# A third landing slab for the first expert stage, in the place of the residual and the position bias

## The chip, the cores and the metric

One core of a Trainium2 chip runs one program: three transformer blocks, one behind the other, on 256 tokens of width 1024, all in float32. The metric is device time in microseconds of one execution. TensorE (PE) multiplies, VectorE (DVE) and ScalarE (ACT) work element by element, GpSimd (POOL) copies and issues some transfers, SyncE (SP) issues the rest.

## The reference, cut to what matters

Block one ends with a mixture of experts: 32 experts, 4 for each token. Block two's attention adds a position bias.

```python
def moe_ffn(h, w_router, b_router, w_mlp1, b_mlp1, w_mlp2, b_mlp2):
    logits = (h @ w_router).astype(jnp.float32) + b_router.astype(jnp.float32)
    top_v, top_i = lax.top_k(logits, TOP_K)
    gates = jax.nn.softmax(top_v, axis=-1)
...
        u = xb @ w_mlp1[e] + b_mlp1[e]
        x_glu = jnp.minimum(u[..., ::2], SWIGLU_LIMIT)
        x_lin = jnp.clip(u[..., 1::2], -SWIGLU_LIMIT, SWIGLU_LIMIT)
        a = x_glu * jax.nn.sigmoid(SWIGLU_ALPHA * x_glu) * (x_lin + 1)
        return a @ w_mlp2[e] + b_mlp2[e]
...
        y = moe_ffn(h.reshape(B * S, D), w_router[l], b_router[l], w_mlp1[l], b_mlp1[l],
                    w_mlp2[l], b_mlp2[l]).reshape(B, S, D)
        x = x + gt2 * rms_norm(y, g_post_ffn[l])
...
        s_c = jnp.einsum('bthd,bnd->bhtn', qb, kc) + tab[:, rel_bucket(dist_c)][None]
```

The second line from the end shows that the residual `x` is needed again only when all experts are summed. `tab[:, rel_bucket(...)]` is the position bias of block two; it depends on no activation.

## The kernel before, in words

**The expert stage.** The 1024x2048 and 1024x1024 weights of one expert are cut into six slabs of 2 MB: 0 to 3 (w_mlp1) and 4, 5 (w_mlp2). Each has one place in SBUF: 0, 1 and 2 in `ring`, 3 in `MOD`, 4 in `HTY`, 5 in `scr`. A place may be loaded again when TensorE has used it in the expert's last pass (semaphore `m1_slab_used[j]`). A pass takes 32 of the expert's tokens; an expert with more has several passes, and all of them need all six slabs. How many passes each expert has is counted on the chip by VectorE (a list that it makes at the stage's start, semaphores `counted` and `listed`); the loops over experts (SP, POOL) and over passes (PE, DVE, ACT) run on those numbers.

Slabs 0 and 1 have a second place each, a landing slab in `scr` (`m1_arrivals`). SP loads the next expert's slabs 0 and 1 there while the present one is still at work, and POOL copies them into `ring` when `m1_slab_used` allows (L712), then tells TensorE by `moved[j]`. SP's order for one expert e is: 2, 3, the bias row, 4, 5 of e, then 0 and 1 of e + 1, each behind its own wait (`next_expert`). One queue carries them in this order.

**One pass on TensorE** (`expert_pass`): up-projection over slabs 0 to 3 (L1111) and the bias row (L1115), the scatter of the pass before (L1148), `back` (L1094), the transposes of the hidden tile (`turn_hidden`, L1124), `gather` for the next pass (L1079), then the down-projection with slabs 4 and 5 (L1137). Between L1115 and L1124 stand, on VectorE, two clamps out of PSUM (L2249, L2250), the multiply by the sigmoid (L2252) and the product with the linear half (L2253), whose result L1124 turns.

**The position bias.** A one-hot product makes one row of 512 distances per head, which ScalarE stores to DRAM (`rel_scratch`). POOL loads windows of it: `BIASR` in one transfer (L689) and `BIASCR` in eight transfers of single elements, every sixteenth (L693). TensorE turns them round with the matrix `flip` in five products (L1021, L1023; plan entry `flip`, behind `gate1`), ScalarE copies the results to `BIAS` and `BIASC`. Block one does not use them.

**Between the expert stage and block two.** POOL waits for the last sum, then loads the parameters of block two (L715 to L720, semaphore `block2_params_landed`, 6 transfers) and clears two areas. TensorE waits for VectorE's new residual (`x1_ready`) and for all six transfers, then turns X (L776) and begins the projections `in2`.

Of the kernel before, what the change touches and what calls it, by code (L numbers as in the profile page):

```python
# [12 lines left out]
P = 128  # L13
S = 256
# [136 lines left out]
def build(nc, I, out, rel_scratch):  # L151
    first, end, first_slab, release = product_plan()
    landed = landed_plan()
    with ExitStack() as ctx:
# [101 lines left out]
        moved, moving = [sem(f"moved{j}") for j in range(2)], sem("moving")  # L256
        early_landed = slab_landed[SLOTS:]
        m1_landed = [sem(f"m1_landed{i}") for i in range(6)]
        m1_row_landed = sem("m1_row_landed")
# [38 lines left out]
        m1_arrivals = [carve(1024 + SLAB * j, 2, 2 * F1) for j in range(2)]  # L298
        b1row, YS = borrow(1024, BANK), borrow(1536, BANK)
# [141 lines left out]
        n_first, n_rel, n_consts = 4, 3, 24  # L441
# [4 lines left out]
        def _(sp):  # L446
# [183 lines left out]
        def _(pool):  # L630
# [16 lines left out]
            with nc.allow_non_contiguous_dma("short vectors"):  # L647
                vector(0)
                const(flip, I["c_flip"], rel_consts_landed)
# [36 lines left out]
            pool.memset(KN, 0.0).then_inc(zeros_ready, 1)  # L686
            pool.wait_ge(rel_stored, 16)
# [7 lines left out]
            vector(3)  # L695

            pool.wait_ge(h2_ready, NT)
            for a in range(NT):
                for half in range(2):
                    r = E1 * (2 * a + half)  # L700
                    pool.dma_start(b2row[r:r + E1, :], I["b_mlp2"][0][:, BANK * half:BANK * (half + 1)]).then_inc(moe1_params_landed, 16)
            for j in range(2):
                pool.wait_ge(early_landed[j], 16 + 16)
                pool.sem_inc(moved[j], 1)
            pool.wait_ge(m1["counted"], 1)
            with pool.Fori(1, E1) as e:
                through = pool.value_load(work[0:1, bass.ds(e + (THROUGH - 1), 1)], min_val=1, max_val=PASSES)
                for j in range(2):
                    pool.wait_ge(m1_landed[j], 16 * e)
                    pool.wait_ge(m1_slab_used[j], through)  # L710
                    pool.sem_inc(moving, 1)
                    pool.tensor_copy(m1_slabs[j], m1_arrivals[j]).then_inc(moved[j], 1)  # L712

            pool.wait_ge(m1["sum"], 1)
# [17 lines left out]
            for j in range(2):  # L732
                pool.wait_ge(early_landed[j], 32 + 32)
                pool.sem_inc(moved[j], 1)
# [11 lines left out]
        def _(pe):  # L746
# [275 lines left out]
            b = bank()  # L1022
            close(pe.matmul(b[:, 0:NT * 4 * NCMP], flip, BIASCR, start=True, stop=True))  # L1023
# [74 lines left out]
            def up(n, e):  # L1098
# [3 lines left out]
                for j in range(4):  # L1102
                    if j < 2:
# [5 lines left out]
                    for i in range(2):  # L1109
                        for c in range(STRIPS1):  # L1110
# [91 lines left out]
            for i in range(4):  # L1202
# [8 lines left out]
                if i in (0, 3):  # L1211
                    tokens(lambda k: wi[:, k, S:2 * S], S)

# [267 lines left out]
        def _(act):  # L1481
# [150 lines left out]
            for i in range(4):  # L1632
                read(BIAS[:, 2 * i:2 * i + 2, :], two(product()))
            read(BIASC[:, :, :, :].rearrange("p t h n -> p (t h n)"), product()[:, 0:NT * 4 * NCMP])
# [96 lines left out]
            read(GH[:, :, :], two(product()), ACT.Sigmoid)  # L1731
            act.wait_ge(conv_gated, 1)
# [130 lines left out]
        def _(dve):  # L1863
# [277 lines left out]

            attention(0, n_window, between_windows)
# [142 lines left out]
            gain_gate(5)  # L2285
            add_gated_norm(Y, 5, m1["sum_read"], NT)
# [51 lines left out]

            attention(n_window, n_window + n_nsa, between_units)
# [224 lines left out]
```

## Time and profile before

| | us |
|---|---|
| runs: median of 3 (lowest, highest) | 2499.62 (2497.68, 2503.69) |
| the profiled execution, its own time | 2493.21 |
| its span in the trace | 2491.4 |
| TensorE busy | 2062.1 (83%) |
| POOL busy | 320.4 (13%) |
| chain that ended last | PE 63%, DMA 22%, DVE 9% |

The three blocks follow one another: the expert stage of block one lies between about 280 and 1283 us of the span, block two follows. Busy shares are means over stages with different limits. A row of the timeline gives start, duration, engine, line, operation and tiles; in brackets stand the idle time before it and what ended it. Names such as `scr<-in_w_mlp` are destination and source.

### The profile page before, as it was taken

Reading aid. Unit: us, or ns where it says so; the run is one execution under the profiler, and the core shown is the slowest. Engines: PE = TensorE matmul, PEld = TensorE weight load, DVE = VectorE, ACT = ScalarE, POOL = GpSimd, SP = SyncE. Lnnn points to the kernel's source line nnn. Section 1 sums busy time; section 2 is a strip of 40 time slices with the busy share of each in tenths; the row PEclk is TensorE's granted clock in tenths of the full one; section 3 lists DMA queues with packets and bytes.
Section 4 is the critical chain, followed back from the end, with each engine's and each line's share of the span. In section 5 each row is a group of like instructions: output and inputs, shape, how many; then the busy total and the mean of one; then the engine's idle time right before and its main releaser. Section 6 shows DMA issues by size and latency. Waiting matters only on the chain.

```text
span 2491.4 us, 34823 instructions
## 1 busy us (share of the span) xinstructions
PE 2062.1 (83%) x14301; PEld 1148.7 (46%) x14302; DVE 521.0 (21%) x1100; ACT 367.3 (15%) x815; POOL 320.4 (13%) x147
## 2 busy tenths in 40 slices
PE   6988589668768966989869788899979899889788
PEld 5765222112212211222228665789965546555444
DVE  1044511001101100111120473110031201241131
ACT  1232111001101100111111422100001112210001
POOL 4100112222222122211220000000000000002221
PEclk9978699889999988999989979999979999989889
DMA  9653679999999799997983635555524334259994
GB/s 322 166 204 140 270 305 401 427 425 409 424 419 408 306 426 426 391 407 311 413 327 136 224 121 200 177 158 144 157 89 139 115 127 161 77 227 383 409 410 162
DMA packets 183290, 681.49 MB, mean 274 GB/s; under 512 B 15954, under 2 KB 57187, under 8 KB 150192
## 3 DMA queue, kind: packets, MB, share of 16 engines
q1 hardware_dynamic: 179200, 670.02, 69.0%
q0 software_dynamic: 4000, 10.37, 1.7%
q8 instruction: 59, 0.97, 0.2%
q14 instruction: 15, 0.12, 0.0%
q10 hardware_dynamic: 16, 0.02, 0.0%
HBM read 679.31 MB, written 1.06 MB: 273 GB/s over the span
## 4 chain that ended last, share of the span: by engine, by line
PE 63%; DMA 22%; DVE 9%; ACT 3%; SPq 2%; issue 1%; POOL 0%; DVEq 0%; ACTq 0%; POOLq 0%
PE ps L765 32%; PE ps L1111 9%; DMA spare<-in_b_mlp 8%; DMA scr<-in_w_mlp 6%; DMA MOD<-in_w_mlp 5%; PE ps L1137 4%; PE ps L1416 2%; PE ps L1148 2%; DMA HTY<-in_w 2%; PE ps L800 2%; PE ps L1115 1%; PE ps L1079 1%; PE ps L1453 1%; DVE scr L2316 1%; PE ps L1427 1%
## 5 line engine op out<-in xcount | busy, mean ns | idle before, releaser
L1111 PE MATMUL ps<-ring,scr 128*32 128x512 f32 x2208 | 286.6, 666 | 133.1 <-POOL ring L712 132.7
L765 PE MATMUL ps<-ring,HTY 128*128 128x512 f32 (+5 forms) x960 | 327.8, 502 | 7.0 <-DMA ring<-in_w_out 3.9
L712 POOL COPY ring<-scr 128x4096 f32<-128x4096 f32 x62 | 224.0, 3617 | 776.2 <-DMA scr<-in_w_mlp 570.1
L765 PEld LDWEIGHTS ps<-ring,HTY 128*128 128x128 f32 x960 | 175.3, 191 | 156.0 <-issue 141.1
L765 PE MATMUL ps<-HTY,ring 128*128 128x256 f32 (+1 forms) x1072 | 238.0, 385 | 1.8 <-ACT HTY L1500 1.8
L1111 PEld LDWEIGHTS ps<-ring,scr 128*32 128x32 f32 x2208 | 72.2, 118 | 342.3 <-POOL ring L712 180.2
L765 PEld LDWEIGHTS ps<-HTY,ring 128*128 128x128 f32 (+1 forms) x1072 | 205.3, 192 | 33.2 <-ACT HTY L1500 2.8
L2249 DVE TENSOR_SCALAR spare<-ps 128x256 f32<-128x256 f32 x46 | 19.5, 424 | 679.4 <-PE ps L1115 679.3
L1500 ACT ACTIVATE scr<-ps 128x512 f32<-128x512 f32 (+6 forms) x118 | 58.4, 497 | 498.3 <-PE ps L765 401.2
L1111 PE MATMUL ps<-MOD,scr 128*32 128x512 f32 x736 | 98.9, 659 | 39.3 <-DMA spare<-in_b_mlp 20.2
L765 PE MATMUL ps<-ring,scr 128*128 128x128 f32 (+1 forms) x1040 | 121.6, 280 | 1.4 <-DVE scr L2355 1.4
L765 PEld LDWEIGHTS ps<-ring,scr 128*128 128x128 f32 x1040 | 117.5, 192 | 5.2 <-issue 3.3
L1674 ACT ACTIVATE spare<-spare 128x256 f32<-128x256 f32 x46 | 19.1, 416 | 597.0 <-DVE spare L2249 597.0
L742 POOL COPY scr<-MOD 128x4096 f32<-128x4096 f32 x7 | 25.2, 3600 | 565.3 <-PE ps L1416 451.9
L1416 PE MATMUL ps<-scr,BIAS 128*32 128x512 f32 x432 | 73.4, 677 | 23.5 <-POOL scr L742 22.8
L1137 PE MATMUL ps<-scr 128*32 128x512 f32 x736 | 88.5, 598 | 5.0 <-DMA scr<-in_w_mlp 5.0
L1148 PE MATMUL ps<-spare,scr 64*128 64x512 f32 x368 | 91.4, 615 | 0.8 <-ACT spare L1684 0.8
L1137 PE MATMUL ps<-HTY,scr 128*32 128x512 f32 x736 | 89.7, 606 | 0.0
L765 PEld LDWEIGHTS ps<-spare,H 128*128 128x128 f32 x320 | 75.4, 329 | 9.2 <-issue 7.5
L765 PE MATMUL ps<-spare,H 128*128 128x128 f32 x320 | 77.3, 402 | 1.6 <-DVE spare L2470 1.6
L1111 PEld LDWEIGHTS ps<-MOD,scr 128*32 128x32 f32 x736 | 24.3, 117 | 104.2 <-issue 64.7
L844 PE MATMUL ps<-ring,cols 128*32 128x128 f32 x1472 | 53.0, 304 | 18.5 <-DMA ring<-in_w_ada 18.5
(443 smaller groups left out, 1982.7 us busy)
## 6 DMA issues: line engine op xcount, KB each, us to landing
scr<-in_w_mlp SPq DMA_DIRECT2D x94, 2048.0 KB, 25.5
ring<-in_w_mlp SPq DMA_DIRECT2D x34, 2048.0 KB, 21.0
MOD<-in_w_mlp SPq DMA_DIRECT2D x32, 2048.0 KB, 24.3
HTY<-in_w_mlp SPq DMA_DIRECT2D x32, 2048.0 KB, 22.2
ring<-in_w_ada SPq DMA_DIRECT2D x23, 2048.0 KB, 9.4
ring<-in_w_in SPq DMA_DIRECT2D x20, 2048.0 KB, 7.9
ring<-in_w_ff SPq DMA_DIRECT2D x16, 2048.0 KB, 9.0
ring<-in_w SPq DMA_DIRECT2D x16, 2048.0 KB, 16.2
```

The costliest lines, as they stand in the source:

```text
L712: pool.tensor_copy(m1_slabs[j], m1_arrivals[j]).then_inc(moved[j], 1)
L742: pool.tensor_copy(m3_slabs[j], m3_arrivals[j]).then_inc(moved[j], 1)
L765: mm = pe.matmul(o, lhs(k), rhs(k), start=begin and k == 0, stop=end and k == nk - 1)
L800: mm = pe.matmul(b[64 * half:64 * half + 64, S * i:S * (i + 1)], c[half](k), rhs[:, k, :], start=k == 0, stop=k == nk - 1)
L844: pe.matmul(b[32 * t:32 * (t + 1), 0:P], csil[:, j, k:k + 1].to_broadcast([P, 32]), w[:, k, P * t:P * (t + 1)], start=k == 0, stop=False)
L1079: mm = pe.matmul(ps[C1 * q:C1 * (q + 1), 3, 0:S], PICK[:, a, :], H[:, a, S * q:S * (q + 1)], start=a == 0, stop=a == NT - 1)
L1111: mm = pe.matmul(ps[C1 * c:C1 * (c + 1), 0, :], XG[:, 2 * j + i, :], m1_slabs[j][:, i, BANK * c:BANK * (c + 1)], start=j + i == 0, stop=False)
L1115: mm = pe.matmul(ps[C1 * c:C1 * (c + 1), 0, :], ones[32 * c:32 * c + 1, 0:C1], b1row[32 * c:32 * c + 1, :], start=False, stop=True)
L1137: mm = pe.matmul(ps[r:r + C1, 1, :], aT[:, i, C1 * c:C1 * (c + 1)], m1_slabs[j][:, 2 * t + i, BANK * half:BANK * (half + 1)], start=j + i ...
L1148: mm = pe.matmul(sum_bank(a, half), GPT[r, P * a:P * (a + 1)], YS[r, :], start=False, stop=last, skip_group_check=True)
L1416: mm = pe.matmul(ps[32 * t:32 * (t + 1), 0, :].rearrange("p (x f) -> p x f", x=2), XG3[:, 4 * h + i, C3 * t:C3 * (t + 1)], m3_slabs[2 * h ...
L1500: act.activation(dst, src, func, **kw).then_inc(product_free, 1)
```

## The change

The residual X and the table BIAS together are as large as one slab. The change makes them a third landing place, for slab 2, in two halves of 1 MB (row pairs k = 0 into X, k = 1 into BIAS). So X is stored to DRAM (`x_scratch`) at the start of the stage and loaded back at its end, and the bias is made in block two: its loads stand on POOL's queue after the last sum, and the plan entry `flip` behind `in2`. SP's order for one expert becomes 3, row, 4, 5 of e, then 0, 1 and the two halves of 2 of e + 1. POOL makes four copies for each expert. VectorE has three waits more (for `rel_stored`, for X, and for `flip` before block two's attention).

```diff
-    ("ada1a", [2] * 4, 0), ("rel", [], 1), ("h1T", [], 4), ("in1", [2, 3, 2, 2, 2], 0), ("gate1", [], 1), ("flip", [], 5),
+    ("ada1a", [2] * 4, 0), ("rel", [], 1), ("h1T", [], 4), ("in1", [2, 3, 2, 2, 2], 0), ("gate1", [], 1),
...
-    ("x1T", [], 4), ("convw", [], 1), ("in2", [4, 3, 2, 2, 2, 2], 0), ("cmp2", [1, 1], 3), ("ada3", [2] * 6, 7), ("ada3b", [2] * 2, 3),
+    ("x1T", [], 4), ("convw", [], 1), ("in2", [4, 3, 2, 2, 2, 2], 0), ("flip", [], 5), ("cmp2", [1, 1], 3), ("ada3", [2] * 6, 7), ("ada3b", [2] * 2, 3),
...
+        m1_half_arrivals = [X.rearrange("p a d -> p (a d)"), BIAS.rearrange("p h s -> p (h s)")]
...
+            def expert_half(e, k, dst, landed=None):
+
+                src = I["w_mlp1"][0][e][4 * P:6 * P, :].rearrange("(p k) n -> p k n", p=P)
+                landed = (m1_landed[2], m1_half_landed)[k] if landed is None else landed
+                sp.dma_start(dst, src[:, k, :]).then_inc(landed, 16)
...
-                for j in (2, 3):
-                    sp.wait_ge(m1_slab_used[j], through)
-                    expert_slab(own, j)
+                sp.wait_ge(m1_slab_used[3], through)
+                expert_slab(own, 3)
...
+                    for k in range(2):
+                        sp.wait_ge(moved[2 + k], e + 1)
+                        expert_half(behind, k, m1_half_arrivals[k])
...
-            expert_slab(0, 2)
+            for k in range(2):
+                expert_half(0, k, m1_slabs[2][:, k, :], early_landed[k])
             sp.wait_ge(h2_ready, NT)
             expert_slab(0, 3)
             expert_row(0)
+            sp.dma_start(x_scratch, X[:, :, :]).then_inc(x_stored, 16)
+            expert_half(1, 1, m1_half_arrivals[1])
             sp.wait_ge(product_ready, end["route1"])
             expert_slab(0, 4)
+            sp.wait_ge(x_stored, 16)
+            expert_half(1, 0, m1_half_arrivals[0])
             sp.wait_ge(m1["counted"], 1)
...
+            sp.wait_ge(moved[2], E1)
+            sp.dma_start(X[:, :, :], x_scratch).then_inc(x_landed, 16)
...
+                for k, landed_half in enumerate((m1_landed[2], m1_half_landed)):
+                    pool.wait_ge(landed_half, 16 * e)
+                    pool.wait_ge(m1_slab_used[2], through)
+                    pool.sem_inc(moving, 1)
+                    pool.tensor_copy(m1_slabs[2][:, k, :], m1_half_arrivals[k]).then_inc(moved[2 + k], 1)
+
+            pool.wait_ge(m1["sum"], 1)
+            pool.dma_start(flip, I["c_flip"]).then_inc(rel_landed, 16)
...
-            pe.wait_ge(rel_landed, 16 * (1 + 4 * NT))
-            for i in range(4):
-                b = bank()
-                close(pe.matmul(b, flip, BIASR[:, 2 * i:2 * i + 2, :], start=True, stop=True))
...
+            dve.wait_ge(x_landed, 32)
             add_gated_norm(Y, 5, m1["sum_read"], NT)
...
+            dve.wait_ge(product_free, end["flip"])
             attention(n_window, n_window + n_nsa, between_units)
```

POOL's queue at the end of the expert stage, before. The first row is the copy of slabs 0 and 1 in the loop over experts; the loads behind the branch are the parameters of block two.

```order
L712 COPY ring<-scr 128x4096 x2
L706 REGISTER_ALU
L706 COMPARE_AND_BRANCH
L715 DMA scr<-in_nsa_cmp_w_2 128x4x64
L716 DMA scr<-in_conv_pw_w 128x2x256
L717 DMA scr<-in_conv_dw_w 31x256
L719 DMA scr<-in_nsa_cmp_b_2 1x16x16 x2
L720 DMA scr<-in_b_ada 48x128
```

The same place of the changed kernel (its lines are numbered anew).

```order
L722 COPY ring<-scr 128x4096 x2
L727 COPY ring<-X 128x2048
L727 COPY ring<-BIAS 128x2048
L716 REGISTER_ALU
L716 COMPARE_AND_BRANCH
L730 DMA scr<-in_c_flip 128x128
L733 DMA scr<-rel_scratch 128x8x256
L737 DMA scr<-rel_scratch 128x15x1 x8
L739 DMA scr<-in_nsa_cmp_w_2 128x4x64
L740 DMA scr<-in_conv_pw_w 128x2x256
L741 DMA scr<-in_conv_dw_w 31x256
L743 DMA scr<-in_nsa_cmp_b_2 1x16x16 x2
```

Two copies are added in the loop, and ten loads now stand ahead of block two's parameters; in the kernel before nine of them followed the loading of constants in block one, and `flip` was among those.

TensorE behind `in1`, before: the gate product (L1016), the five flip products, and the first scores of attention (L881).

```order
L1016 MATMUL ps<-scr,wgu 128x256 x2
L1021 MATMUL ps<-scr 128x512 x4
L1023 MATMUL ps<-scr 128x120
L881 MATMUL ps<-spare,scr 128x256 x4
L844 MATMUL ps<-ring,cols 32x128 x32
```

And TensorE of the changed kernel behind the last product of `in2` (L789), ahead of the products `cmp2` (L1249), where the five now stand.

```order
L789 MATMUL ps<-HTY,ring 128x256 x32
L1237 MATMUL ps<-scr 128x512 x4
L1239 MATMUL ps<-scr 128x120
L1249 MATMUL ps<-ring,scr 15x128 x32
L1252 MATMUL ps<-scr,ones 15x128 x2
```

The five products moved from between the gate and the first scores to between `in2` and `cmp2`.

## Rows read from the trace of the kernel before

**Rows 1.** Windows: busy us (x instructions) of PE, PEld, DVE, ACT, POOL; clock, DMA share, GB/s

```profile
405.00:1255.00 850.00, 659.83 (x5178) 198.72 (x5170) 117.18 (x312) 99.28 (x234) 193.03 (x55) 0.92 0.96 400
825.00:855.00 30.00, 28.87 (x252) 9.51 (x248) 5.51 (x16) 5.09 (x12) 7.14 (x2) 1.00 0.43 173
```

**Rows 2.** Timeline of POOL, copies of slab 0 of two experts that follow

```profile
642.28 3.60 POOL L712 COPY ring<-scr 128x4096 f32<-128x4096 f32 x1 [21.14 <-DMA scr<-in_w_mlp]
...
671.95 3.60 POOL L712 COPY ring<-scr 128x4096 f32<-128x4096 f32 x1 [21.27 <-DMA scr<-in_w_mlp]
```

**Rows 3.** Timeline of SP, issue of slab 2 and slab 4 after a long hole

```profile
842.83 0.34 SPq L489 DMA_DIRECT2D ring<-in_w_mlp  x1
...
851.58 0.39 SPq L491 DMA_DIRECT2D HTY<-in_w_mlp  x1
```

**Rows 4.** Timeline of an expert's end, its slab-1 copy beside VectorE's multiply

```profile
585.59 3.60 POOL L712 COPY ring<-scr 128x4096 f32<-128x4096 f32 x1 [1.20 <-DMA scr<-in_w_mlp]
...
586.56 2.90 DVE L2252 TENSOR_TENSOR spare<-spare 128x256 f32<-128x256 f32 x1
...
589.98 0.51 PE L1124 MATMUL ps<-ident,spare 128*128 128x128 f32 x2 [2.24 <-DVE spare L2253]
```

**Rows 5.** Timeline at the stage's start, VectorE's list of passes beside POOL's first copies

```profile
283.42 8.17 POOL L712 COPY ring<-scr 128x4096 f32<-128x4096 f32 x2 [22.23 <-issue]
...
284.39 3.73 DVE L2234 TENSOR_TENSOR spare<-spare,rows 128x1056 f32<-128x1056 f32 x1
...
298.93 0.70 PE L1124 MATMUL ps<-ident,spare 128*128 128x128 f32 x2 [10.48 <-DVE spare L2253]
...
304.68 0.40 SPq L491 DMA_DIRECT2D HTY<-in_w_mlp  x1
```

**Rows 6.** Timeline of an expert's end where both slabs had landed early

```profile
839.46 7.14 POOL L712 COPY ring<-scr 128x4096 f32<-128x4096 f32 x2 [36.13 <-PE ps L1111]
...
848.17 0.48 PE L1124 MATMUL ps<-ident,spare 128*128 128x128 f32 x2 [0.56 <-ACT scr L1670]
```

**Rows 7.** Timeline after the last sum: parameters of block two, turn of X

```profile
1282.34 0.80 POOL L715 DMA_DIRECT2D scr<-in_nsa_cmp_w  x1 [21.00 <-PE ps L1148]
...
1285.38 0.51 POOL L720 DMA_DIRECT2D scr<-in_b_ada  x1
...
1294.40 1.97 PE L776 MATMUL ps<-ident,X 128*128 128x128 f32 x8 [12.38 <-DVEq L2287]
```

**Rows 8.** Timeline of POOL in block one, loads of the bias; last, line L693's landing

```profile
55.55 0.90 POOL L689 DMA_DIRECT2D scr<-rel_scratch  x1
...
68.58 5.97 POOL L693 DMA_DIRECT2D scr<-rel_scratch  x5 [9.73 <-issue]
83.53 1.20 POOL L693 DMA_DIRECT2D scr<-rel_scratch  x1 [8.97 <-issue]
84.73 0.56 POOL L645 DMA_DIRECT2D spare<-in_g_post_ffn  x1
...
DMA to landing us min/median/max: 7.0/8.2/16.0
```

**Rows 9.** Window over those loads, columns as in rows 1

```profile
70.00:76.00 6.00, 6.00 (x30) 5.28 (x29) 0.00 (x0) 0.60 (x1) 4.55 (x4) 1.00 0.91 56
```

**Rows 10.** Timeline: flip products on TensorE, the first scores read by VectorE

```profile
113.19 2.84 PE L1021 MATMUL ps<-scr 128*128 128x512 f32 x6
119.28 1.84 PE L1021 MATMUL ps<-scr 128*128 128x512 f32 x2 [3.25 <-ACT BIAS L1500]
120.91 0.62 PE L1023 MATMUL ps<-scr 128*128 128x120 f32 x2
...
120.26 1.42 DVE L2111 TENSOR_TENSOR_SCAN scr<-ones,scr 128x256 f32<-128x256 f32 x2
...
123.28 0.88 DVE L1978 SCALAR_TENSOR_TENSOR scr<-ps,window 128x256 f32<-128x256 f32 x2 [1.61 <-PE ps L881]
```

**Rows 11.** Timeline of TensorE behind `in2`

```profile
1393.47 2.75 PE L1222 MATMUL ps<-ring,scr 128*15 128x128 f32 x24 [4.13 <-DVE scr L2296]
```

More of the change, by code:

```diff
@@ L255, in build @@
         m1_slab_used = [sem(f"m1_slab_used{j}") for j in range(6)]
-        moved, moving = [sem(f"moved{j}") for j in range(2)], sem("moving")
+        moved, moving = [sem(f"moved{j}") for j in range(4)], sem("moving")
         early_landed = slab_landed[SLOTS:]
         m1_landed = [sem(f"m1_landed{i}") for i in range(6)]
+        m1_half_landed, x_stored = sem("m1_half_landed"), sem("x_stored")
         m1_row_landed = sem("m1_row_landed")
@@ L439, in slot @@
             return shaped(places[place(s)][:, off:off + k * n], (k, n))
-        n_first, n_rel, n_consts = 4, 3, 24
+        n_first, n_rel, n_consts = 4, 2, 24
         first_gains = (2, 3, 0, 1)
@@ L648, in _ @@
                 vector(0)
-                const(flip, I["c_flip"], rel_consts_landed)
                 const(onehot, I["c_onehot"], rel_consts_landed)
@@ L686, in _ @@
             pool.memset(KN, 0.0).then_inc(zeros_ready, 1)
+            vector(3)
+            pool.wait_ge(h2_ready, NT)
+            for a in range(NT):
+                for half in range(2):
+                    r = E1 * (2 * a + half)
+                    pool.dma_start(b2row[r:r + E1, :], I["b_mlp2"][0][:, BANK * half:BANK * (half + 1)]).then_inc(moe1_params_landed, 16)
+            for j in range(2):
+                pool.wait_ge(early_landed[j], 16 + 32)
+                pool.sem_inc(moved[j], 1)
+                pool.sem_inc(moved[2 + j], 1)
+            pool.wait_ge(m1["counted"], 1)
+            with pool.Fori(1, E1) as e:
+                through = pool.value_load(work[0:1, bass.ds(e + (THROUGH - 1), 1)], min_val=1, max_val=PASSES)
+                for j in range(2):
+                    pool.wait_ge(m1_landed[j], 16 * e)
+                    pool.wait_ge(m1_slab_used[j], through)
+                    pool.sem_inc(moving, 1)
+                    pool.tensor_copy(m1_slabs[j], m1_arrivals[j]).then_inc(moved[j], 1)
+                for k, landed_half in enumerate((m1_landed[2], m1_half_landed)):
+                    pool.wait_ge(landed_half, 16 * e)
+                    pool.wait_ge(m1_slab_used[2], through)
+                    pool.sem_inc(moving, 1)
+                    pool.tensor_copy(m1_slabs[2][:, k, :], m1_half_arrivals[k]).then_inc(moved[2 + k], 1)
+            pool.wait_ge(m1["sum"], 1)
+            pool.dma_start(flip, I["c_flip"]).then_inc(rel_landed, 16)
             pool.wait_ge(rel_stored, 16)
@@ L694, in _ @@
                             .then_inc(rel_landed, 16)
[L695 to L714, printed above, removed]
             pool.dma_start(cw2, I["nsa_cmp_w2_2"][0].rearrange("a (c p) n -> p a c n", p=P)).then_inc(block2_params_landed, 16)
@@ L732, in _ @@
             for j in range(2):
-                pool.wait_ge(early_landed[j], 32 + 32)
+                pool.wait_ge(early_landed[j], 48 + 32)
                 pool.sem_inc(moved[j], 1)
@@ L1017, in _ @@
             close(mm)
-            pe.wait_ge(rel_landed, 16 * (1 + 4 * NT))
-            for i in range(4):
-                b = bank()
-                close(pe.matmul(b, flip, BIASR[:, 2 * i:2 * i + 2, :], start=True, stop=True))
-            b = bank()
-            close(pe.matmul(b[:, 0:NT * 4 * NCMP], flip, BIASCR, start=True, stop=True))
             def rest_of_modulation(i):
@@ L1102, in up @@
                 for j in range(4):
-                    if j < 2:
+                    if j < 3:
                         pe.wait_ge(moved[j], e + 1)
@@ L1109, in up @@
                     for i in range(2):
+                        if 2 * j + i == 5:
+                            pe.wait_ge(moved[3], e + 1)
                         for c in range(STRIPS1):
@@ L1212, in _ @@
                     tokens(lambda k: wi[:, k, S:2 * S], S)
+            pe.wait_ge(rel_landed, 16 * (2 + 4 * NT))
+            for i in range(4):
+                b = bank()
+                close(pe.matmul(b, flip, BIASR[:, 2 * i:2 * i + 2, :], start=True, stop=True))
+            b = bank()
+            close(pe.matmul(b[:, 0:NT * 4 * NCMP], flip, BIASCR, start=True, stop=True))
             pe.wait_ge(blocks_ready, 1)
@@ L1631, in _ @@
             log_sigmoid_part(GL[:, :, :], GZ[:, :, :])
-            for i in range(4):
-                read(BIAS[:, 2 * i:2 * i + 2, :], two(product()))
-            read(BIASC[:, :, :, :].rearrange("p t h n -> p (t h n)"), product()[:, 0:NT * 4 * NCMP])
             def rest_of_modulation(i):
@@ L1731, in _ @@
             read(GH[:, :, :], two(product()), ACT.Sigmoid)
+            for i in range(4):
+                read(BIAS[:, 2 * i:2 * i + 2, :], two(product()))
+            read(BIASC[:, :, :, :].rearrange("p t h n -> p (t h n)"), product()[:, 0:NT * 4 * NCMP])
             act.wait_ge(conv_gated, 1)
@@ L2140, in between_windows @@
                     merge(0, end["ada1b"])
+            dve.wait_ge(rel_stored, 16)
             attention(0, n_window, between_windows)
```

1 line of the change is left out of this document (added).

## The prediction

> **What bounds the kernel now.** I read the page first: TensorE is busy 83% of the span and the chain of work that ended last gives 22% to transfers. An average over three blocks says little about one stage, so I cut the first expert stage out by windows. From 405 to 1255 us the 16 DMA engines are busy 96% and move 400 GB/s [rows 1]. The reader is to see two regimes. In the first, POOL begins the copy of slab 0 every 29.6 us [rows 2]: six slabs of 2.10 MB in that time are 425 GB/s, and TensorE waits for transfers. In the second, an expert has two or more passes, every buffer is full, and DMA runs dry. At 425 GB/s the 850 us could have moved 6% more, so DMA is idle for 850 x 25/425 = 50 us; one long hole holds 17.8 of it (30 us at 173 GB/s) [rows 1], and the other, from 1140 to 1170, is like it. A third landing slab is aimed at these 50 us.
>
> **Part 1, the landing slab: what it can give.** When a pass frees buffers, SyncE issues slab 2 (842.83) and, 8.75 us later, slab 4 (851.58) [rows 3]; slab 3 goes between them. DMA needs 4.93 us a slab (29.6/6), so slabs 2 and 3 keep it busy for 9.86 us, and slab 4 starts 1.1 us after it could have by its own wait. In the changed kernel slab 2 is already in the residual's and the bias' place. DMA then restarts on slab 3, which ends before slab 4 may be issued. What follows the hole (slabs 4 and 5, then 0 and 1 of the next expert) is tied to slab 4's buffer, that is to TensorE's last use of it. The lead of 4.93 us is spent inside the hole; only 1.1 us per hole comes out. I count eleven ends of expert with full buffers. At most eight of them pass on to DMA a restart that is set by slabs 2 and 3, and where the next expert also has several passes TensorE alone sets the pace and nothing is gained.
>
> **Part 2, the landing slab: what it costs.** Each expert now gets four POOL copies: two of 3.60 us and two halves, by size 1.8 us each. While transfers are the bound they are hidden: they end 3.6 + 3.6 = 7.2 us after slab 1 landed, slab 3 lands after 9.9. At the end of a multi-pass expert they are not. The vector multiply at L2252 reads two SBUF tiles. In most passes it takes 0.42 us; in seven it takes more, 2.90 in the one shown, and each time it ends 0.27 us after POOL's copy (585.59 + 3.60; 586.56 + 2.90) [rows 4]. So it waits for POOL. The next instruction, L2253, also reads two SBUF tiles, and TensorE's transposes at L1124 wait for it: in that pass they sat idle 2.24 us. With a half copy queued behind slab 1's copy, L2252 slips in between (at 284.39 a waiting vector instruction did just that: it ended at 288.12, inside POOL's pair, and the pair took 8.17 us instead of 7.14 [rows 5, 6]). Then the half goes, and L2253 waits 1.8 us for it. No row shows L2253 itself beside a copy: bounds are nothing (it waits for nobody) and 3.6 us (both halves first). I take 1.8, by the nearest row, L2252, which has the same kinds of operands.
>
> The Trainium skill speaks against the change here (SBUF — State Buffer, "Who interferes with whom"): "A DVE instruction with two SBUF inputs contends with a GpSimd instruction that reads SBUF", and whichever starts first keeps the shared port for its whole instruction. By that rule L2253 waits as L2252 does; the trace agrees for L2252 with its 2.90 us. Were the rule limited to L2252, the loop term below would be -2 instead of +14.
>
> The ledger of the loop, by ends of expert. (a) Four with both copies back to back, like 839.46: L2252 just escapes, and the transposes at 848.17 have waited for ScalarE, so 0.8 us of the 1.8 is slack [rows 6]: 1.0 lost, 1.1 gained, about 0; at the first of them the next expert is TensorE's again and there is no gain: +1.0. (b) Seven where L2252 already waits, like 585.59: no slack. In two of them (near 585 and 676) slab 4 already set the restart: +1.7 each. In two more 1.1 and 1.4 remain after the gain. Three are followed or made by multi-pass experts in a row (1023 to 1090): 1.8, 1.4 and 0.3. Sum of (b): 9.4. (c) The start. There the pair at 283.42 stands beside VectorE's list of passes; L2234 took 3.73 us, and L1124 waited 10.48 us for VectorE, slab 4 of expert 1 being issued only at 304.68 [rows 5]. Two more halves, 2 x 1.8 us, meet the rest of that list, some fifteen short instructions from L2236 to L2258, nearly all with two SBUF tiles or a copy from SBUF to SBUF: +3.5, with DMA idle meanwhile, so it is passed on whole. Loop: 1.0 + 9.4 + 3.5 = **+14 us**; bounds -2 (L2253 free) and +23 (eleven times 1.8, plus 3.5, no gain).
>
> Hidden at nothing: the store of the residual (1.05 MB) and expert 1's halves, in the DMA hole before 304.68; and the reload, queued behind the last expert's slab 5, while VectorE adds the residual only after the last sum, where POOL too moves on at 1282.34 [rows 7] (2.5 us of transfer; without that cover it costs those 2.5).
>
> **Part 3, the bias moves to block two.** (a) Its ten loads now stand on POOL's queue after the sum and *ahead* of the six that TensorE waits for before it turns X. Before, these were issued from 1282.34 to 1285.9 and TensorE turned X at 1294.40, having waited for VectorE alone [rows 7]. In block one POOL needed 29.2 us from the window load at 55.55 to its next work at 84.73: the eight loads of single elements pause twice, 9.73 and 8.97 us [rows 8]. That is issue only; from 70 to 76 DMA is busy 91% at 56 GB/s [rows 9], so these loads also hold the engines. Low bound: no pause. 1282.34 + 0.56 + 0.90 + 8 x 1.20 = 1293.4, the last parameter load 3.0 later, landing at least 7.0: 1303.4, +9. High bound: both pauses, landing 16.0 [rows 8]: 1282.9 + 29.2 + 3.0 + 16.0 = 1331, +37. Between: from 68.58 to 83.53 five loads drained before POOL moved again, 3.0 us each; eight are 24, the window load 2.5 at 425 GB/s, from 1283.8 to 1310.3, and the parameters land 7.0 later: 1317.3. TensorE begins 22.9 later than now: **+23 us**. Nothing gives it back: behind TensorE stand ScalarE's reads, and the next slabs are released by its products. (b) Five flip products in block one go. They ran from 113.19, and VectorE's first score read came at 123.28 instead of at 121.7, when its scan ended [rows 10]: **-1.5**. (c) They return after in2, where TensorE sits idle 4.13 us for VectorE [rows 11]; they need 2.84 + 1.84 + 0.62 = 5.3 [rows 10]: **+1.2**. Without that hole it would be 5.3.
>
> **Sum.** 14 + 23 - 1.5 + 1.2 = 36.7 us. The profiled execution took 2493.21 (span 2491.4 and 1.8 around it), so it would take 2529.9. It is 6.4 under the median of the runs shown, 2499.62; forecast as such a median: **2536.3**.
>
> **Rivals.** *L2253 waits for nobody* (0.16). For it: no row shows it beside a copy. Against: its operands. Loop -2: 2520.5. *POOL's queue runs through* (0.13). For it: in block one 24 constants stood in the queue ahead of these loads; here none do. Against: the second pause came after only five loads. Params +9: 2522. *The lead is kept* (0.05): a stall is shortened by a whole slab, 4.93 us in each of three long holes (the third lies near 360) and the short ones whole, 50 - 2 x 17.8 = 14.4: 29 us; with 3.5, 23, 1.2 and -1.5 beside it 2497, not slower. It needs slab 4 not to be tied to TensorE's last use. Against: 851.58 less 842.83 is only 8.75. It decides once more than 26 us come out. *The wait for parameters nears its high bound* (0.08): 2552 and up.
>
> **Numbers.** My forecast has 0.58, and its own range is 2524 to 2548. The range 2514 to 2552 takes in both milder rivals and leaves out the kept lead and the high bound, some 0.15. A change of 0.3% (7.5 us) can be told from none: slower 0.94, within it 0.03, faster 0.03.
>
> **What would show it.** TensorE's turn of X after a wait of more than 20 us that ends on a parameter load; POOL's eight element loads with one or two pauses after the sum; L2252 at 0.4 and L2253 late by about 1.8 in passes with a half copy; slab 4 of expert 1 issued near 308 (less 1.5); the holes as long in TensorE's time but with 2.1 MB less to load after them. I am wrong if the element loads drain in a few us, or if the time from one slab-4 issue to the next shrinks by more than 2 us at the end of multi-pass experts.

## The result and the profile after

| | before | after |
|---|---|---|
| median, us | 2498.65 | 2531.32 (2524.12 to 2532.87) |
| ratio | | 1.0133, 95% interval 1.0116 to 1.0150 |
| the profiled execution, its span | 2493.21, 2491.4 | 2531.37, 2529.6 |

The change makes the kernel 1.3% slower. The forecast was 2536.3, in a range from 2514 to 2552.

The page of the changed kernel: busy times, and three groups of its fifth part.

```profile
PE 2075.8 (82%) x14301; PEld 1153.5 (46%) x14302; DVE 541.5 (21%) x1100; ACT 367.6 (15%) x815; POOL 438.8 (17%) x209
...
L722 POOL COPY ring<-scr 128x4096 f32<-128x4096 f32 x62 | 223.8, 3617 | 673.3 <-DMA scr<-in_w_mlp 486.8
...
L1144 PE MATMUL ps<-ident,spare 128*128 128x128 f32 x92 | 22.9, 332 | 58.6 <-DVE spare L2281 39.4
```

POOL is busy 118 us more (its half copies take 61.3 and 60.8), which by itself costs nothing. The last row does: TensorE's transposes (L1144, before L1124) now wait 39.4 us for VectorE's L2281, where they waited 18.4 for L2253 before; their whole wait grew from 41.0 to 58.6. Next, windows over the same 850 us as [rows 1], with the same columns.

```profile
405.00:1255.00 850.00, 660.25 (x5132) 195.85 (x5125) 131.56 (x304) 96.72 (x228) 297.51 (x108) 0.92 0.94 393
```

The third landing slab was to fill the gaps between transfers, and DMA moves less than before: 393 GB/s for 400.

**An expert's end with several passes**, answering to [rows 4]: POOL, VectorE and TensorE of the changed kernel.

```profile
589.00 3.60 POOL L722 COPY ring<-scr 128x4096 f32<-128x4096 f32 x1 [1.29 <-DMA scr<-in_w_mlp]
592.54 2.08 POOL L727 COPY ring<-X 128x2048 f32<-128x2048 f32 x1
594.57 2.08 POOL L727 COPY ring<-BIAS 128x2048 f32<-128x2048 f32 x1
...
589.97 2.90 DVE L2280 TENSOR_TENSOR spare<-spare 128x256 f32<-128x256 f32 x1
592.91 1.99 DVE L2281 SCALAR_TENSOR_TENSOR spare<-spare 128x256 f32<-128x256 f32 x1
...
594.96 0.70 PE L1144 MATMUL ps<-ident,spare 128*128 128x128 f32 x2 [3.82 <-DVE spare L2281]
```

The reader is to see a chain of hand-overs. L2280 ends at 592.87, 0.27 after slab 1's copy; the first half starts at 592.54; L2281 ends at 594.90, again 0.28 after that copy. An instruction of 0.42 us lasts nearly as long as its neighbour. TensorE's wait grew from 2.24 to 3.82.

The wait has a tail. Windows over the 35 products that follow it, first here, then at the same end in the kernel with late copies (below), where TensorE waits 0.56:

```profile
594.96:599.50 4.54, 4.54 (x35) 1.56 (x35) 0.82 (x3) 0.77 (x2) 1.69 (x1) 0.66 0.49 208
```

```profile
584.17:587.30 3.13, 3.13 (x35) 1.23 (x35) 1.58 (x1) 0.77 (x2) 3.13 (x2) 1.00 1.04 442
```

The third number from the end is TensorE's granted clock, a share of 2.4 GHz: 0.66 behind the long wait, 1.00 without it. The same products take 1.4 us more.

And the end where both slabs had landed early, answering to [rows 6] and [rows 3].

```profile
848.26 7.14 POOL L722 COPY ring<-scr 128x4096 f32<-128x4096 f32 x2 [32.35 <-PE ps L1131]
855.35 2.16 POOL L727 COPY ring<-X 128x2048 f32<-128x2048 f32 x1
...
855.79 1.99 DVE L2281 SCALAR_TENSOR_TENSOR spare<-spare 128x256 f32<-128x256 f32 x1
...
857.84 0.51 PE L1144 MATMUL ps<-ident,spare 128*128 128x128 f32 x2 [1.34 <-DVE spare L2281]
...
853.44 0.33 SPq L492 DMA_DIRECT2D MOD<-in_w_mlp  x1
...
861.29 0.39 SPq L494 DMA_DIRECT2D HTY<-in_w_mlp  x1
```

Here 0.56 of the wait is the usual one for ScalarE, so 0.78 is lost. DMA restarts on slab 3 at 853.44 and slab 4 follows 7.85 later, still tied to TensorE.

**The start**, answering to [rows 5]: VectorE's list of passes beside four copies, and slab 4 of expert 1.

```profile
283.64 8.17 POOL L722 COPY ring<-scr 128x4096 f32<-128x4096 f32 x2 [21.91 <-issue]
291.76 1.89 POOL L727 COPY ring<-X 128x2048 f32<-128x2048 f32 x1
293.60 1.89 POOL L727 COPY ring<-BIAS 128x2048 f32<-128x2048 f32 x1
...
291.90 1.80 DVE L2266 TENSOR_SCALAR spare<-spare,stat 128x66 f32<-128x66 f32 x1
293.73 1.83 DVE L2267 TENSOR_TENSOR spare<-spare 128x66 f32<-128x66 f32 x1
...
308.34 0.41 SPq L494 DMA_DIRECT2D HTY<-in_w_mlp  x1
```

Each half stretches one short instruction (0.32 and 0.23 us before) to its own length.

**The end of the stage**, answering to [rows 7]: POOL's loads, then TensorE's turn of X.

```profile
1294.91 0.57 POOL L730 DMA_DIRECT2D scr<-in_c_flip  x1 [17.47 <-PE ps L1168]
1295.48 0.92 POOL L733 DMA_DIRECT2D scr<-rel_scratch  x1
1296.38 8.38 POOL L737 DMA_DIRECT2D scr<-rel_scratch  x7
1318.42 1.20 POOL L737 DMA_DIRECT2D scr<-rel_scratch  x1 [13.66 <-issue]
1319.62 0.76 POOL L739 DMA_DIRECT2D scr<-in_nsa_cmp_w  x1
...
1322.63 0.51 POOL L744 DMA_DIRECT2D scr<-in_b_ada  x1
...
1328.17 3.65 PE L800 MATMUL ps<-ident,X 128*128 128x128 f32 x16 [33.57 <-issue]
```

Seven loads of single elements go through, the eighth waits 13.66, and the six parameters stand behind it. TensorE is idle 33.57 us where it was idle 12.38.

**In block one**, where the flip products stood ([rows 10]): TensorE, then a window of 119 to 126 us of before and of after (0.50 is the lower of the two levels, 1.2 GHz, for the whole window).

```profile
122.64 2.08 PE L905 MATMUL ps<-spare,scr 128*128 128x256 f32 x4 [8.32 <-DVE scr L2005]
124.65 3.06 PE L868 MATMUL ps<-ring,cols 128*32 128x128 f32 x64
```

```profile
119.00:126.00 7.00, 5.68 (x40) 3.47 (x44) 4.57 (x11) 3.72 (x9) 0.00 (x0) 0.76 0.04 13
```

```profile
119.00:126.00 7.00, 3.36 (x32) 2.43 (x36) 4.75 (x12) 2.78 (x10) 0.00 (x0) 0.50 0.04 15
```

### The profile page after: what moved, and what is told of

It is laid out like the page before. It is cut to its first block, busy times and chain, and to the rows that moved or that the text cites. A ratio compares the mean times of both kernels' runs of the same rounds, so it can differ in the third digit from the quotient of the medians.

```text
span 2529.6 us, 35042 instructions
## 1 busy us (share of the span) xinstructions
PE 2075.8 (82%) x14301; PEld 1153.5 (46%) x14302; DVE 541.5 (21%) x1100; ACT 367.6 (15%) x815; POOL 438.8 (17%) x209
## 4 chain that ended last, share of the span: by engine, by line
PE 61%; DMA 22%; DVE 9%; ACT 3%; issue 2%; SPq 2%; POOL 0%; DVEq 0%; ACTq 0%; POOLq 0%
PE ps L789 32%; DMA scr<-in_w_mlp 17%; PE ps L1131 7%; PE ps L1157 5%; PE ps L1443 2%; DMA spare<-in_b_mlp 2%; PE ps L824 2%; DMA HTY<-in_w 1%; PE ps L1097 1%; PE ps L1168 1%; PE ps L1135 1%; PE ps L1480 1%; PE ps L1454 1%; PE ps L868 1%; PE ps L930 1%
## 5 line engine op out<-in xcount | busy, mean ns | idle before, releaser
L1131 PE MATMUL ps<-ring,scr 128*32 128x512 f32 x2208 | 296.7, 682 | 134.8 <-POOL ring L722 128.2
L789 PE MATMUL ps<-ring,HTY 128*128 128x512 f32 (+5 forms) x960 | 328.0, 503 | 7.0 <-DMA ring<-in_w_out 4.0
L789 PEld LDWEIGHTS ps<-ring,HTY 128*128 128x128 f32 x960 | 175.3, 191 | 156.2 <-issue 141.3
L789 PE MATMUL ps<-HTY,ring 128*128 128x256 f32 (+1 forms) x1072 | 238.1, 385 | 1.8 <-ACT HTY L1527 1.8
L789 PEld LDWEIGHTS ps<-HTY,ring 128*128 128x128 f32 (+1 forms) x1072 | 205.4, 192 | 33.2 <-ACT HTY L1527 2.7
L2277 DVE TENSOR_SCALAR spare<-ps 128x256 f32<-128x256 f32 x46 | 19.5, 425 | 670.2 <-PE ps L1135 670.2
L789 PE MATMUL ps<-ring,scr 128*128 128x128 f32 (+1 forms) x1040 | 121.6, 280 | 1.4 <-DVE scr L2385 1.4
L789 PEld LDWEIGHTS ps<-ring,scr 128*128 128x128 f32 x1040 | 117.5, 192 | 5.2 <-issue 3.3
L1131 PE MATMUL ps<-MOD,scr 128*32 128x512 f32 x736 | 89.3, 603 | 20.2 <-DMA spare<-in_b_mlp 14.8
L789 PEld LDWEIGHTS ps<-spare,H 128*128 128x128 f32 x320 | 75.4, 329 | 9.2 <-issue 7.5
L789 PE MATMUL ps<-spare,H 128*128 128x128 f32 x320 | 77.3, 402 | 1.6 <-DVE spare L2500 1.6
L1144 PE MATMUL ps<-ident,spare 128*128 128x128 f32 x92 | 22.9, 332 | 58.6 <-DVE spare L2281 39.4
```

The costliest lines, as they stand in the source:

```text
L789: mm = pe.matmul(o, lhs(k), rhs(k), start=begin and k == 0, stop=end and k == nk - 1)
L1131: mm = pe.matmul(ps[C1 * c:C1 * (c + 1), 0, :], XG[:, 2 * j + i, :], m1_slabs[j][:, i, BANK * c:BANK * (c + 1)], start=j + i == 0, stop=False)
```

## Three intervals that make all runs comparable

Executions of one kernel differ by some 10 us, and half of that arises before the expert stage: POOL's first copy begins anywhere from 278.6 to 284.1 us in kernels that have the same code up to there. So I cut each profiled execution at three points: POOL's first copy, POOL's first load after the last sum, and TensorE's turn of X; the rest is up to the end of the span. The first row comes out of [rows 5, 7], the second from the rows above (1294.91 - 283.64, 1328.17 - 1294.91, 2529.6 - 1328.17), the others in the same way from their traces.

| kernel | expert stage | load to turn | turn to end | median, us | ratio (95%) |
|---|---|---|---|---|---|
| before | 998.92 | 12.06 | 1197.0 | 2498.65 | |
| after | 1011.27 | 33.26 | 1201.4 | 2531.32 | 1.0133 |
| e1_loads_last | 1011.25 | 12.07 | 1199.2 | 2507.65 | 1.0042 (1.0028, 1.0057) |
| e2_bias_only | 1000.74 | 31.59 | 1203.4 | 2515.80 | 1.0070 (1.0053, 1.0087) |
| e3_halves_late | 990.21 | 33.01 | 1202.2 | 2507.99 | 1.0043 (1.0029, 1.0057) |
| e4_copies_late | 980.22 | 32.66 | 1202.4 | 2498.68 | 1.0005 (0.9993, 1.0016) |
| e5_both | 979.88 | 12.06 | 1203.3 | 2475.79 | 0.9922 (0.9904, 0.9940) |
| e6_before_late | 989.37 | 12.06 | 1200.9 | 2483.15 | 0.9949 (0.9930, 0.9967) |
| e7_four_loads | 1011.32 | 24.09 | 1200.8 | 2518.13, one run | |
| e8_both_clock | 979.91 | 12.06 | 1199.8 | 2486.14 | 0.9956 (0.9940, 0.9972) |
| e9_psum_operand | 994.47 | 33.36 | 1198.2 | 2511.42 | 1.0057 (1.0042, 1.0072) |
| e10_both_clock_7 | 979.69 | 12.06 | 1199.8 | 2478.38 | 0.9917 (0.9902, 0.9932) |

The reader is to see how sharp the first two columns are, and where they are not. Kernels that share the stage's code agree within 0.1 us (1011.25 to 1011.32) and 0.6 us (979.69 to 980.22), whatever their whole times do. But e2_bias_only has the stage's code of before and takes 1.8 us more (1000.74 for 998.92): of its seven stalls of L2252 five last 2.87 to 2.89 us, in before only two do. So what is measured against the stage of before is known to some 2 us. The runs beside which each kernel was timed had medians of 2497.50 (e1 to e4), 2496.63 (e5 to e8) and 2497.63 (e9, e10).

## The experiments

**Is it the queue ahead of the parameters?** In the changed kernel the bias loads were moved behind the parameters and the clears.

```diff
-            pool.dma_start(flip, I["c_flip"]).then_inc(rel_landed, 16)
...
             for area in (BD, KN):
                 pool.memset(area, 0.0).then_inc(zeros_again, 1)
+            pool.dma_start(flip, I["c_flip"]).then_inc(rel_landed, 16)
...
```

> The changed kernel, only the ten loads of the bias moved on POOL's queue: behind block two's six parameters and the two clears. Theory (parameters late because they queue behind the element loads, issue and transfer together): TensorE's turn of X again waits for VectorE, near 1307 instead of 1328.17, so 21 us come back: about 2510. The bias is then made under in2's 95 us, and TensorE does not wait for it ahead of the flip products. Rival (the same transfers only delay something else later, such as the weights of in2): less than half comes back, 2520 or more, with waits for weights between 1310 and 1400. Rival (the turn waits for something else, such as the reload of X): no change, 2531.

TensorE's turn of X stands at 1302.18 after 12.38 us for VectorE; the interval is 12.07 as before, and the stage is the same. The eighth load still pauses (11.18 us), with nobody behind it who matters. The wait costs 33.26 - 12.07 = 21.2 us and nothing is taken elsewhere.

**Does the move of the bias cost this without the landing slab?** The kernel before with part 3 of the change alone.

```diff
             pool.wait_ge(m1["sum"], 1)
+            pool.dma_start(flip, I["c_flip"]).then_inc(rel_landed, 16)
...
             pool.dma_start(cw2, I["nsa_cmp_w2_2"][0].rearrange("a (c p) n -> p a c n", p=P)).then_inc(block2_params_landed, 16)
```

> The kernel before with only the bias moved to block two, its loads ahead of the parameters as in the changed kernel; no third landing slab, no store or reload of X. Theory (the two halves of the change add up): parameters +21, block one +0.5 (the 1.5 gained turns into a loss because TensorE's clock falls), blocks two and three +4.4: 26 slower than before, about 2525. The element loads pause near 13.7 us again. Rival (the wait of 33.6 us ahead of the turn comes from the landing slab, whose reload and last transfers are in the way of the loads): under 15 slower, 2513 or less.

Load to turn 31.59, which is 19.5 more than before (the pause was 12.21). The whole is 18 us slower, not 26: I had put 4.4 into blocks two and three and 0.5 into block one from one pair of profiles, and no cost of that size shows. The last column runs from 1197.0 to 1203.4 in the twelve kernels whatever their code there, and e6_before_late, whose code there is that of before, has 1200.9. The rival is out.

**Is it L2281 beside the halves, and L2280 beside slab 1?** POOL waits for the expert's last hidden tile before the halves, and in the second kernel before slab 1's copy already.

```diff
+                pool.wait_ge(m1["hidden"], through)
                 for k, landed_half in enumerate((m1_landed[2], m1_half_landed)):
```

```diff
                     pool.wait_ge(m1_slab_used[j], through)
+                    if j == 1:
+                        pool.wait_ge(m1["hidden"], through)
```

> The changed kernel, with POOL waiting for VectorE's L2281 of the expert's last pass (semaphore hidden) before it copies the two halves; slabs 0 and 1 as before. Theory (L2281 waits for the copy of the first half, and TensorE for L2281): all L2281 take 0.42 us, where twelve took 1.99; 12 x 1.57 = 18.8 less the slack in five of them (0.8 each) and less what slab 4's restart then gives up, and the start gives back its 3.5: about 15 come out of the loop, 2516. Rival (L2281's wait is hidden; what costs is the split of a slab into two transfers, or POOL being late with the halves): within 4 of 2531.

> As the run with late halves, but POOL waits for hidden already before the copy of slab 1, so that no copy but slab 0's can stand beside L2280 and L2281. Theory (L2280's stalls of 0.45 to 2.5 us in seven passes, which the kernel before has too, cost TensorE as much): another 8 to 10 us, 2507, and L2280 takes 0.42 throughout. Rival (the copies then come too late for TensorE's next up-projection): TensorE waits for moved at slab 1 or 2, and the time is that of the late halves or worse.

With late halves the stage loses 21.1 us (1011.27 to 990.21), more than the 15 expected; L2281 is never longer than 0.43 (it was 1.99 eleven times; my expectation says twelve, a miscount). With slab 1's copy late as well another 10.0 us go, to 980.22, and both take 0.42 throughout. TensorE does not wait for the later copies at these ends. VectorE's L2281 and TensorE at the end shown above, in the kernel with both edits (L2283, L1146 there), beside the late copies:

```profile
580.39 3.60 POOL L724 COPY ring<-scr 128x4096 f32<-128x4096 f32 x1 [3.40 <-DVE spare L2283]
583.93 2.08 POOL L729 COPY ring<-X 128x2048 f32<-128x2048 f32 x1
...
579.71 0.42 DVE L2283 SCALAR_TENSOR_TENSOR spare<-spare 128x256 f32<-128x256 f32 x1
582.53 1.73 DVE L2207 TENSOR_TENSOR spare<-spare 128x256 f32<-128x256 f32 x1 [2.40 <-PE ps L1099]
```

The copy now follows L2283 at once. What is stretched in its place is L2207 (0.43 to 1.73), for which no other engine waits.

**Is it that both inputs lie in SBUF?** Copies as in the changed kernel; L2281 reads one input from PSUM.

```diff
-                    pe.wait_ge(m1["up_read"], n)
+                    pe.wait_ge(m1["hidden"], n)
...
-                tell(dve.scalar_tensor_tensor(aS, lin1, 1.0, sig, ALU.add, ALU.mult), m1["hidden"], n + 1)
+                tell(dve.scalar_tensor_tensor(aS, ps[:, 0, 1:BANK:2], 1.0, sig, ALU.add, ALU.mult), m1["hidden"], n + 1)
```

> The changed kernel, only L2281 reads the linear half from PSUM, so that it has one SBUF input instead of two (the clamp L2278 still runs, but its limit at 7 is left out of the product; TensorE frees the bank at hidden instead of at up_read). POOL's copies stay as they are. Theory (it waits because both its inputs are in SBUF, as POOL's copy is): L2281 takes 0.42 to 0.5 also beside a half copy, L2280 still waits 2.9 beside slab 1's; the loop is as with the late halves, about 20 us shorter, 2511. Rival (any vector instruction, or any that writes SBUF, waits for the copy): L2281 stays at 1.99 in twelve passes, 2531.

The same end of expert in this kernel: POOL, and VectorE's two instructions.

```profile
582.15 3.60 POOL L722 COPY ring<-scr 128x4096 f32<-128x4096 f32 x1 [1.29 <-DMA scr<-in_w_mlp]
585.70 2.09 POOL L727 COPY ring<-X 128x2048 f32<-128x2048 f32 x1
...
583.12 2.90 DVE L2280 TENSOR_TENSOR spare<-spare 128x256 f32<-128x256 f32 x1
586.06 0.42 DVE L2281 SCALAR_TENSOR_TENSOR spare<-ps,spare 128x256 f32<-128x256 f32 x1
```

L2280, with both inputs in SBUF, still takes 2.90 beside slab 1's copy. L2281, with one, runs in 0.42 in the middle of the half copy at 585.70. On VectorE only the place of one operand was changed (with it TensorE's release of the bank came later, and the clamp dropped out of the product), and 16.8 us of the stage went (1011.27 to 994.47; I had expected 20). That is the price of the eleven waits. The trace agrees with the rule that the prediction quoted of the Trainium skill (SBUF — State Buffer, "Who interferes with whom"): with two inputs in SBUF the instruction waits, 2.90 us, and with one it does not, 0.42.

**What the third slab gives when it is not in the way.** The kernel before, with the wait ahead of slab 1's copy (the second diff above), and the changed kernel with both edits.

> The kernel before, two landing slabs, with only the wait for hidden ahead of slab 1's copy. Theory (L2252's stalls beside slab 1's copy, 10.4 us over seven passes, stand on TensorE's path): L2252 takes 0.42 in all passes, the loop is 8 us shorter, 2490; what the third slab itself gives is then the rest of the 18.7 us that the late copies took out of the loop of before, about 10. Rival (the stalls were slack, or slab 1 then comes late): within 3 of before, and the third slab has given nearly all of the 18.7.

> The changed kernel with both edits: slab 1's copy and the two halves behind hidden, and the bias loads behind the parameters. Theory (two causes, in different stages, that add): the loop as with the late copies, 980.2 us from POOL's first copy to the last sum (998.9 before), and TensorE's turn of X 12.1 behind POOL's first load: 33 and 21 us less than the changed kernel, about 2477, faster than the kernel before by 21. Rival (block two was short of POOL or of DMA time either way): more than 2487.

Before gains 9.6 us of stage and 0.5% of its time from one line. The third slab then gives 9.5 more (989.37 to 979.88), and in the whole time 2483.15 to 2475.79. The kernel with both edits is 0.8% faster than the kernel before and 2.2% faster than the change. Its DMA in the stage:

```profile
405.00:1240.00 835.00, 662.47 (x5162) 196.12 (x5158) 140.06 (x308) 98.12 (x231) 298.41 (x110) 0.91 0.97 406
```

**Issue or transfer?** Four of the eight element loads are left out, and with them half of `BIASCR`; TensorE waits for four loads fewer, and its last flip product reads `BIASR` instead. The kernel serves for this interval alone.

```diff
-                for t in range(NT):
+                for t in range(1):
                     for h in range(4):
```

> The changed kernel with four of the eight loads of single elements (half of BIASCR is left out, and the last flip product reads other data). Theory (the loads hold the DMA engines as well as POOL's queue): POOL does not pause, the parameters are issued 19 us earlier, but land only when the four have drained, at 3.0 each: the turn of X waits for parameters until about 15 us behind POOL's first load, some 18 earlier than with eight loads, and 3 later than without them. Rival (only the pause of the queue cost time): the turn waits for VectorE alone, 12.1 behind the first load. Second rival (the pause is not a matter of how many loads stand there): a pause of 9 or more among or behind the four.

POOL does not pause: the last parameter is issued at 1300.67, 9.3 us behind the first load (with eight 27.7), yet TensorE turns X only at 1315.48. Load to turn is 24.09: half of the loads keep 12.0 of the 21.2 us. From 1300 to 1305 DMA is busy and moves little:

```profile
1300.00:1305.00 5.00, 0.00 (x0) 0.00 (x0) 2.10 (x2) 0.00 (x0) 5.00 (x8) 0.50 1.00 76
```

So the rival that only the queue's pause cost time is out. My own number for this run, 15, was too low: I had counted the elements alone, and in the same stretch stand the window load of 1 MB and slabs of in2 (368 GB/s from 1310 to 1316).

**Did the clock eat the 1.5 us of block one?** Filler products where the flip products stood, on top of both edits; first fifteen, then seven.

```diff
+            b = bank()
+            for i in range(15):
+                pe.matmul(b, ident[:, :], X[:, 0, 0:BANK], start=True, stop=True)
```

> As the run with both edits, and in block one, where the flip products stood, 15 products of the same size into a bank that nobody reads before its next product overwrites it. Theory (without the flip products TensorE is idle for 8.3 us and its granted clock falls to 0.50 from 119 to 126, where it was 0.76; this turned the 1.5 us gained into 0.5 lost): the clock stays above 0.9 there, L868's first 64 products take 1.95 where they took 3.06, and TensorE is about 2 us earlier by 130. In the whole time 2 us are below what the ratio can tell. Rival (the loss is from the order of TensorE and ScalarE, not from the clock): the clock rises, and the time by 130 stays as it is or gets later.

> As the run with both edits and filler products in block one, but seven products instead of fifteen: each has two entries in the trace and takes 0.88 us, so that fifteen took 13.1 us and delayed the first scores by 6.5; seven take 6.1, inside TensorE's 8.3 idle us. Theory (the clock ate the 1.5 us): granted clock 1.00 from 119 to 126 instead of 0.50, L870's first 64 products take 1.95, and TensorE is 1 to 2 us earlier at the second group of them than with both edits alone; in the whole time no difference that the ratio can tell, 2474 against 2476. Rival (what the clock is granted between 130 and 280 depends on how TensorE stood before, and undoes it): POOL's first copy comes as late as in the run with fifteen, 14.8 us behind that with both edits, or anywhere between.

Fifteen were a mistake of size: they took 13.14 us and pushed the first scores behind VectorE. By 154 us VectorE was 5.2 late, by 192 it was 6.9, and POOL's first copy came 14.8 late; most of the rest fell where the clock from 190 to 220 was 0.66 instead of 0.89. Behind the fifteen the first 64 products took 1.95, so at that place the clock was kept. Seven fit:

```profile
113.63 6.28 PE L1047 MATMUL ps<-X,ident 128*128 128x512 f32 x14
119.74 1.03 PE L907 MATMUL ps<-spare,scr 128*128 128x256 f32 x4
123.09 1.13 PE L907 MATMUL ps<-spare,scr 128*128 128x256 f32 x4 [2.32 <-DVE scr L2011]
124.15 3.46 PE L870 MATMUL ps<-ring,cols 128*32 128x128 f32 x64
```

```profile
119.00:122.50 3.50, 1.77 (x7) 0.83 (x5) 3.01 (x6) 1.46 (x2) 0.00 (x0) 1.00 0.13 51
122.50:128.00 5.50, 4.91 (x76) 3.87 (x76) 3.31 (x10) 1.74 (x9) 0.00 (x0) 0.69 0.01 3
```

The filler kept the clock at 1.00 to 122.5 and it fell right after: the 64 products took 3.46, longer than without filler. From the gate product to the second group of 64 it is 16.96 us, with both edits alone 17.01, before 16.91. My theory that seven products give the 1.5 us back fails; with them the low stretch moved and did not go. POOL's first copy stands at 284.65, 4.2 behind both edits alone, as the rival allowed. The time shows nothing (2478.38 and 2475.79, intervals overlapping).

## Why the prediction was right, step by step

- **The loop, +14: measured +12.35** (1011.27 - 998.92; 10.5 against e2_bias_only, with the same stage as before), and in the main from the right parts. *The start*, +3.5: the first to the second copy of slab 0 took 43.87 us for 40.44, +3.4 (42.21, 43.56 and 43.82 in e1, e7 and e9, whose copies there are the same); with late halves it is 40.41. *The waits*: eleven, as counted, at 1.57 each instead of 1.8, since L2281 took 1.99 and needs 0.42; 0.78 instead of 1.0 where ScalarE's result leaves slack. By the kernel with the PSUM operand they cost 16.8; my eleven less slack were 7 x 1.8 + 4 x 1.0 = 16.6. That these two agree is in part luck: with the sizes measured the sum is 7 x 1.57 + 4 x 0.78 = 14.1. What it lacks, and the prediction had at nothing, is *the clock behind a long wait*. At the five ends where TensorE waited 2.87 to 3.82 us, it took 4.95 to 6.38 us from the transposes to the second half of the down-projection, where it takes 3.59 at full clock: 9.2 in all. With the PSUM operand these ends lost 5.0, in before 1.7. TensorE's wait for the hidden tile is 11.8 less with the PSUM operand (58.6 and 46.8), the slow products 4.2 less: 16.0 of the 16.8. *What the slab gives back*: 20.2 less 12.35 is 7.9; the ledger had 6.1 in it. With no copy in VectorE's way it gives 9.5, of at most 8 x 1.1 = 8.8 that I had allowed. The lead of a whole slab is not kept: 31 ends of expert give 9.5 us, less than two slabs' 4.93.
- **Single ends** were less good than their sum. By the times of slab 0's copies the two ends near 369 and 401 bring -0.9, those at 839 and 1159 -0.8 each, where I had +1.0 for the four (the -0.9 is one long interval of before, 45.46, for 44.5 in every other kernel). The seven others bring +9.9 for 9.4, but as 1.4, 2.9, 1.1, 3.3, 0.8, -0.4 and 0.9: the sum is right, and luck has a part in it. At two of them (1063 and 1096 now) the early slab put both copies back to back, so that L2280 escapes. Between the ends, where transfers are the bound, another 1 us is lost in all, which I had at nothing: slab 0's copies stand 29.69 us apart where they stood 29.53 to 29.62. The seventh transfer is not the cause: e2_bias_only and e6_before_late, with six, show up to 29.69 and 29.70 too. The cause stays open.
- **The parameters, +23: measured 21.2.** From POOL's first load to the last parameter's issue it is 27.7 us, where I had 28.0 until the eight had drained; TensorE turned X 5.5 later instead of 7.0. The one pause was 13.66, the two of block one 9.73 and 8.97. That the loads hold DMA as well as the queue was the right middle value: four of them without any pause still cost 12.0.
- **The flip products leaving block one, -1.5: wrong.** VectorE's first read of scores did come at 121.70, 1.6 earlier, but TensorE, idle 8.32 us, was granted 0.50 of its clock from 119 to 126 (0.76 before); its next 64 products took 3.06 instead of 1.95, and the second 64 began at 129.54, where before had them at 129.07. What I priced was the read and not the clock of the engine behind it. In the other kernels with the same code there the first 64 took 2.66 to 3.21, and from the gate product to the second 64 it is 16.98 to 17.54, for 16.91 before. So the term is +0.1 to +0.6.
- **Their return behind in2, +1.2: measured +0.4**: cmp2 started 34.15 later than before, the turn 33.77. They ran at full clock in 3.8 us.

```profile
1423.28 3.60 PE L1237 MATMUL ps<-scr 128*128 128x512 f32 x8
...
1427.62 3.67 PE L1249 MATMUL ps<-ring,scr 128*15 128x128 f32 x64 [0.53 <-DVE scr L2325]
```

- **Store and reload of X, at nothing: right.** e1_loads_last, which stores and reloads X, turns it 12.07 us behind POOL's first load, before 12.06; and with late halves the start, beside the store, takes 40.41 for 40.44.
- **The sum.** 12.35 + 21.2 + 0.2 (first copy) + 4.4 (turn to end) = 38.2 us between the spans, against 36.7. The 4.4 are the place where I had 1.2; by the column of all kernels, it cannot be told from scatter of the executions that were profiled. The medians differ by 32.7, where loop and parameters make 33.6: the profiled execution of before is 5.4 under its median, that of after is at it. Of the rivals, the free L2253, the queue that runs through and the kept lead are each excluded by a measurement (1.99 in L2281, 13.66 of pause, 9.5 us from the slab, which is compared between two single executions); the high bound did not come.

## What to carry to other kernels

A background copy on POOL costs what it meets on VectorE: before adding one, list the instructions with two SBUF inputs that can run beside it and whose result TensorE waits for, and start the copy after them, or read one input from PSUM. Count with the wait what the clock takes behind it: here the 35 products after a wait of 3.82 us took 4.54 us instead of 3.13. Here one added semaphore wait gave 9.6 us without the landing slab and 31 with it, and turned the slab's 12 us of loss into 9.5 of gain over a kernel before that has the same wait. Loads of single elements go last on a queue, behind everything that somebody waits for: here they held the queue (13.66 us of pause) and the DMA engines (busy 100% at 76 GB/s). A deeper buffer is worth only the part of a stall that does not hang on the next buffer in line; here 9.5 us, where 50 us of idle DMA had seemed to be there.

## What the runs showed of the hardware

- A waiting vector instruction with two SBUF inputs slips in between two POOL copies. L2280 ended at 592.87; the half copy behind it is recorded from 592.54 and is longer for it (2.08 to 2.17 us at the ends where VectorE slips in, 1.89 elsewhere).
- Short vector instructions stretch too: 66 columns took 1.80 and 1.83 beside a half, and in the kernel with both edits a copy of two columns (0.17) took 0.92.
- The granted clock between 190 and 220 us differs from execution to execution of the same instructions, and more than half of the 5 us of scatter ahead of the expert stage arises there. The changed kernel, then the kernel with the PSUM operand, which is 2.4 us ahead at 190, 5.4 at 205, and whose first copy came 5.0 earlier:

```profile
190.00:220.00 30.00, 21.17 (x236) 19.13 (x235) 15.08 (x24) 8.28 (x17) 0.00 (x0) 0.74 0.29 99
```

```profile
190.00:220.00 30.00, 20.86 (x236) 16.45 (x236) 15.07 (x24) 7.95 (x14) 0.00 (x0) 0.89 0.48 179
```

- In the nine kernels that have the eight loads of 128 x 15 single elements behind the stage, POOL's queue paused once for 10.9 to 13.9 us, ahead of the eighth; with four there was no pause.
